# Attention in pairs of heads on the two row halves of the matmul array, with PSUM laid out anew

## The reference

```
z = RMSNorm(x) @ W_in                    # split into qA kA vA qB kB vB
A: 8 q heads, 2 kv heads, head dim 64, own 64-row chunk + 2 chunks before, learned sink per head
B: 8 heads, head dim 64, own chunk + 8 chunks before, learned bias by relative distance
s = q k^T / 8 (+ bias), masked;  m = max(s, sink);  p = exp(s - m) / (sum + exp(sink - m))
x = x + W_out @ concat(RMSNorm_a(p_A v_A), RMSNorm_b(p_B v_B))
x = x + MoE(RMSNorm(x))                  # top-1 of 4 groups, then top-2 of 8 gated experts, FF 256
```

## Time and profile before

| | us |
|---|---|
| three timed runs | 1059.56, 1064.88, 1090.57 (median 1064.88) |
| the profiled execution | 1060.6 |
| its span, first to last instruction | 1058.8 |
| PE, DVE, ACT busy in the span | 1010.7, 395.1, 299.8 |
| mean granted clock of PE | 0.99 |

### The profile page before, as it was taken

How to read it: one execution, slowest core, us unless ns; L and a number is a source line. 1 busy time by engine, 2 the same in 40 slices (tenths; PEclk the granted TensorE clock), 3 DMA queues, 4 the chain that set the end, 5 groups by cost and what they waited for, 6 DMA issues and landing times. The chain is left out here.

```text
span 1058.8 us, 16244 instructions
## 1 busy us (share of the span) xinstructions
PE 1010.7 (95%) x6187; PEld 521.7 (49%) x6187; DVE 395.1 (37%) x1155; ACT 299.8 (28%) x866; POOL 89.3 (8%) x72
## 2 busy tenths in 40 slices
PE   6999999999899999999999999998999999988995
PEld 3444555454485455465655556578544333333331
DVE  0343233342555546364555546358231111111110
ACT  1221222221435435353544535220111111111110
POOL 1000000000200000000000000000221221111111
PEclk9999999999999999999999999999999999999998
DMA  9510111100281101011010301076589999999972
GB/s 356 196 40 1 40 40 40 40 13 27 100 300 45 60 1 61 13 48 39 23 60 1 148 33 60 2 301 257 204 298 353 391 389 387 389 387 388 383 267 41
DMA packets 34439, 164.64 MB, mean 155 GB/s; under 512 B 7808, under 2 KB 9888, under 8 KB 20928
## 3 DMA queue, kind: packets, MB, share of 16 engines
q1 hardware_dynamic: 24192, 134.92, 32.1%
q0 software_dynamic: 6912, 17.32, 6.6%
q10 hardware_dynamic: 3264, 11.44, 2.8%
HBM read 147.10 MB, written 24.41 MB: 162 GB/s over the span
## 5 line engine op out<-in xcount | busy, mean ns | idle before, releaser
L1260 PE MATMUL ps<-arena 128*128 128x512 f32 (+1 forms) x640 | 252.2, 554 | 8.2 <-DMA arena<-in_w_in 8.2
L1260 PEld LDWEIGHTS ps<-arena 128*128 128x128 f32 x640 | 121.4, 191 | 133.9 <-issue 129.6
L1510 PE MATMUL ps<-arena 128*32 128x512 f32 x1536 | 171.9, 598 | 10.6 <-DMA arena<-in_wexp 9.2
L1342 PE MATMUL ps<-arena 64*128 64x256 f32 (+4 forms) x384 | 123.2, 421 | 0.0
L1423 PE MATMUL ps<-arena 128*128 128x512 f32 x256 | 120.6, 592 | 0.0
L942 DVE COPY arena<-ps 128x128 f32<-128x128 f32 (+2 forms) x144 | 53.7, 373 | 166.4 <-PE ps L1354 165.5
L784 ACT ACTIVATE arena<-arena 128x256 f32<-128x256 f32 (+6 forms) x144 | 84.0, 583 | 90.0 <-DVE arena L1027 89.7
L1510 PEld LDWEIGHTS ps<-arena 128*32 128x32 f32 x1536 | 49.9, 110 | 114.9 <-issue 113.0
L1342 PEld LDWEIGHTS ps<-arena 64*128 64x128 f32 x384 | 59.0, 185 | 74.4 <-DVE arena L1027 46.3
L1528 PE MATMUL ps<-arena 128*32 128x512 f32 x768 | 87.2, 592 | 0.7 <-ACT arena L841 0.7
L1023 DVE CUSTOM_DVE_ANT_0 arena<-ps,arena 128x256 f32<-128x256 f32 (+6 forms) x144 | 77.5, 538 | 2.6 <-PE ps L1342 1.9
(11 more groups left out here) (162 smaller groups left out, 870.0 us busy)
## 6 DMA issues: line engine op xcount, KB each, us to landing
arena<-in_wexp SPq DMA_DIRECT2D x96, 1024.0 KB, 24.6
arena<-in_x SPq DMA_DIRECT2D x18, 512.0 KB, 4.5
arena<-in_w_in ACTq DMA_DIRECT2D x3, 2048.0 KB, 23.0
arena<-in_xT SPq DMA_DIRECT2D x9, 512.0 KB, 3.6
arena<-in_w_out SPq DMA_DIRECT2D x1, 4096.0 KB, 13.9
out_y<-arena SPq DMA_DIRECT2D x8, 512.0 KB, 2.6
h_rows<-arena SPq DMA_DIRECT2D x8, 512.0 KB, 3.0
arena<-in_bias SPq DMA_DIRECT2D x1, 2560.0 KB, 9.1
```

What stands on the lines that cost most here:

```text
L1260: ins = mm(bank(Z_BANK[c], 0, CHUNK[c]), xt[:, j, k, :], w_in[:, a:a + CHUNK[c]], start=(k == 0), stop=(k == KD - 1))
L1342: ins = mm(ps[:, at:at + step], q, kt[:, col:col + step], start=True, stop=True)
L1510: ins = mm(bank(s % 2)[u:u + UNIT], xgt[:, s % 2, k, u:u + UNIT], ring[expert_of(s, q) % RING][:, k * 512:(k + 1) * 512], start=(k == 0), ...
```

## The change

Units run over t, then pairs of heads, then m, then the two heads of the pair: two units in a row are two heads of one mixer, and v counts the 72 pairs. The heads of A are paired over the two kv heads (h and h+4), with sinks, gains and w_out's rows reordered on the host. `scores(v)` makes both heads' scores, alternately from partitions 0 to 63 and 64 to 127, into different banks; A and B share banks 1 and 2, and where one of them is over 512 wide the scores wait for all earlier biasing. PSUM: banks 0 to 3 scores, 4 and 5 transposed probabilities (4 also the pair's output, transposed back), 7 the values' sum, 6 alone the stage behind, except in the last tiles. Each pair is divided at once; each head has its own exp of the sink.

```diff
+        o_ps = bank(4, 3 * P, 4 * P)
+        pv_ps = bank(7, 0, P)
+        def scores_at(m, r, width):
+            if m == 0:
+                return (640, 1024)[r]
+            return 0 if r == 0 else 2048 - max(width, 512)
...
-        units = [(t, m, h) for t in range(NT) for h in range(HEADS) for m in (0, 1)]
+        units = [(t, m, 2 * p + r) for t in range(NT) for p in range(4) for m in (0, 1) for r in range(2)]
...
-        BUSY = ({19: 22, 21: 3, 22: 2}, {7: 2, 9: 3, 19: 20, 21: 9, 22: 8})
+        BUSY = ({21: 20, 23: 3, 24: 2}, {9: 2, 12: 3, 21: 20, 23: 9, 24: 8})
...
 ACT
+            for v in range(NV + 3):
+                pair_out(v - 3)
+                copy_pt(2 * v - 2)
+                probs(2 * v + 2)
+                if v % 8 == 3 and v >= 8:
+                    squares_out(v // 8 - 1)
+                pieces(act_pieces, 2 * v)
+                copy_pt(2 * v - 1)
+                probs(2 * v + 3)
+                pieces(act_pieces, 2 * v + 1)
             squares_out(NT - 1)
...
 DVE
+            def divide(v):
+                dve.wait_ge(s_p, 2 * v + 2)
...
+                    link(nc.vector.reciprocal(r2, s2))
+                dve.wait_ge(s_ob, v + 1)
+                dve.wait_ge(s_pt, min(2 * v + 6, NU))
...
-                if g in (13, 17):
+                if g in (15, 18):
...
+            for v in range(NV + 3):
+                copy_pt(2 * v - 2)
+                biased(2 * v + 2)
+                pieces(dve_pieces, 2 * v)
+                divide(v - 3)
+                copy_pt(2 * v - 1)
+                biased(2 * v + 3)
+                if v % 8 == 3 and v >= 8:
+                    norm_out(v // 8 - 1)
+                pieces(dve_pieces, 2 * v + 1)
             norm_out(NT - 1)
...
 PE
+            def scores(v):
...
+                if v >= 1:
+                    wide = unit_info(2 * v - 1 if m == 0 else 2 * v)[5] > 512
+                    if wide or v >= 2:
+                        pe.wait_ge(s_sp, 2 * v if wide else 2 * v - 2)
...
+                for i in range(len(runs)):
+                    for r in range(2):
+                        a = r * HD
...
+                        ins = mm(ps[:, at:at + step], q, kt[:, col:col + step], start=True, stop=True)
+                        if i == len(runs) - 1:
+                            ins.then_inc(s_qk[r], 1)
...
+                pe.wait_ge(s_ott, v + 1)
+                pe.wait_ge(s_ptv, min(2 * v + 5, NU))
+                if v >= 1:
+                    pe.wait_ge(s_on, v)
+                nc.tensor.transpose(o_ps, outt[:, v % 2], ident).then_inc(s_ob, 1)
...
+                if t < NT - 1 and g in (12, 13, 14, 16, 17, 18):
+                    n = (g - 12) // 4
+                    at = g - 12 - 4 * n
...
+                    if g == 16:
+                        pe.wait_ge(s_x2, 2 * t + 1)
+                    for c in range(3 * at, min(3 * at + 3, KD)):
+                        ins = mm(bank(6), ot[:, c], w_out[:, c, 512 * n:512 * n + 512], start=(c == 0), stop=(c == KD - 1))
...
+                if g in (21, 22):
+                    half = g - 21
+                    if half == 0:
+                        pe.wait_ge(s_h2, t + 1)
+                    elif t < NT - 2:
+                        pe.wait_ge(s_h2a, t + 1)
...
+            for v in range(NV + 3):
...
+                transpose_probs(2 * v - 2)
+                scores(v + 1)
+                pieces(pe_pieces, 2 * v)
+                pair_back(v - 3)
+                transpose_probs(2 * v - 1)
+                pieces(pe_pieces, 2 * v + 1)
+                values(v - 2)
+                if 1 <= v < FIRST_OUT:
+                    keep_busy(5 - v // 4, 6)
```

More of the change, by code:

```diff
@@ L772, in act_pieces @@
                     rstd(rs2, ss2).then_inc(s_s2, 1)
-                if g == 20:
+                if g == 21:
                     act.wait_ge(s_t2, 2 * t + 1)
                     nc.scalar.activation(h2t[:, 0:4], bank(6).rearrange("p (g c) -> p g c", g=4), ACT.Copy).then_inc(s_h2a, 1)
[L777 to L794, removed]
-                copy_pt(u)
-            pair_out(NU - 1)
+            probs(0)
+            probs(1)
+            for v in range(NV + 3):
[8 more added lines that the diff above has]
+                pieces(act_pieces, 2 * v + 1)
             squares_out(NT - 1)
-            for u in range(NU, NU + 24):
+            for u in range(NU + 6, NU + 25):
                 pieces(act_pieces, u)
@@ L954, in divide @@
[L954 to L962 removed]
+                    dve.wait_ge(s_pv[u % 2], u // 2 - 1)
@@ new lines, in copy_pt @@
+                assert all(x[2] == P for x in tiles[:cut])
+                nc.vector.tensor_copy(pt_of(u)[:, 0:cut * P], bank(4, 0, cut * P)).then_inc(s_ptv, 1)
+            def divide(v):
+                if not 0 <= v < NV:
+                    return
+                t, m, h = units[2 * v]
+                c = stat_at(m, h)
+                dve.wait_ge(s_p, 2 * v + 2)
+                r2, s2 = rden[:, c:c + 2], psum_e[:, t % 2, c:c + 2]
+                if m == 0:
+                    dve.wait_ge(s_es, v + 2)
+                    link(nc.vector.tensor_tensor(r2, s2, esink[:, h:h + 2], ALU.add))
+                    link(nc.vector.reciprocal(r2, r2))
+                else:
+                    link(nc.vector.reciprocal(r2, s2))
+                dve.wait_ge(s_ob, v + 1)
+                dve.wait_ge(s_pt, min(2 * v + 6, NU))
+                a = 512 * m + h * HD
+                nc.vector.tensor_tensor(row[:, t, a:a + P].rearrange("p (h c) -> p h c", c=HD),
+                                        o_ps.rearrange("p (h c) -> p h c", c=HD),
+                                        r2.unsqueeze(2).broadcast_to([P, 2, HD]), ALU.mult).then_inc(s_on, 1)
@@ L1004, in dve_pieces, with biased @@
                     ins.then_inc(s_lt, 1)
-                if g == 23:
+                if g == 24:
                     dve.wait_ge(s_lg, t + 1)
-                    nc.vector.tensor_tensor(logits[:, t], bank(7, 0, NR), rbias, ALU.add).then_inc(s_rv, 1)
-            for u in range(NU):
+                    nc.vector.tensor_tensor(logits[:, t], bank(6, 256, 256 + NR), rbias, ALU.add).then_inc(s_rv, 1)
+            def biased(u):
+                if u >= NU:
+                    return
                 t, m, h, segs, tiles, width = unit_info(u)
-                k = u % 16
                 c = stat_at(m, h)
@@ L1028, in _ @@
                                         ALU.mult).then_inc(s_sp, 1)
[L1029 to L1048 removed]
+            biased(0)
+            biased(1)
+            for v in range(NV + 3):
[8 more added lines that the diff above has]
+                pieces(dve_pieces, 2 * v + 1)
             norm_out(NT - 1)
[L1050 to L1051 removed]
             dve.wait_ge(s_rload, 16 * 10)
@@ L1095, in choose_second @@
                 tt_(mb[:, t0:t1], eq_, wide(c_valid[:, t0:t1].unsqueeze(2), NE), ALU.mult).then_inc(s_mb, 1)
-            for u in range(NU + 10, NU + 24):
+            for u in range(NU + 6, NU + 25):
                 pieces(dve_pieces, u)
```

287 lines of the change are left out of this document (117 added, 170 removed).

## The result

The changed kernel takes 1050.6 us (median of four runs, 1049.8 to 1052.4) for 1064.5 before; the ratio is 0.989 (95% interval 0.986 to 0.992). It is a ratio of means, without one execution of before that ran in a slower state (1090.6 us). 1050 was predicted, and no difference beyond 2%. Its profiled execution took 1051.3 us, span 1049.5, mean granted clock 0.97.

The account below looks back on a forecast made before the run. It took attention to be bound by PE's own instruction stream. With serial waits counted, tiles 1 to 3 gave -4.6, -2.3, -2.8, four steady tiles -1.3 each, the drain +4.1: -10.8 us from 1060.6, so 1050, range 1016 to 1084.

Parts of the forecast that it names:

- Term 1: Score passes on PE: even and odd heads stream together on two row halves, 83 us becoming 42, 41 us less work.
- The fear for runs of 128 columns: Weight loads leave these runs no gain; each of 16 wide B pairs would lose 0.2 us, 3 us in all.
- Term 2: Switches to the half-array form on PE: 72 visits instead of 144, 0.26 us each, 19 us saved, bounds 14 and 26.
- PE's own work: PE's instruction stream in attention falls by 60 us of 392; a steady tile from 49.1 to about 41.
- Term 3: Attention turns: new serial waits on DVE and ACT give time back; steady tiles take 47.8 us, gaining 1.3, not 8.
- Term 4: Drain from tile 8 to its transposes: w_out, residual chain and fillers come later, 64.5 us for 60.4, 4.1 us lost.
- The third rival: PE's clock falls in the new waits: 28 us slower, 1078 us; chance 0.05.
- The first rival: DVE's and ACT's turns hide behind PE, so only PE's work counts: 1005 us, or 1028 with half the waits; chance 0.21.
- The second: Rival: row halves take turns on PE instead of overlapping while the waits stay: 1087 us; chance 0.12.

Follow-up runs that it names:

- the parted run: Changed kernel with a full-array filler product between all even-head and all odd-head score passes of each pair: 1107.4 us, ratio 1.042 to the kernel before.
- e9: e7 plus, in the turn behind the squares, DVE's h2 moved ahead of the even head's bias: 1038.4 us, ratio 0.975 to the kernel before.
- the two drain runs: Changed kernel with 4 fillers instead of 20 ahead of tile 7's h2 transposes: 1045.9 us; with DVE's norm of tile 8's mixer also moved later: 1043.5 us.
- e10: e9 plus 4 fillers instead of 20 ahead of tile 7's h2 transposes and DVE's late norm: 1033.0 us, ratio 0.971 to the kernel before.
- e4: Changed kernel with eight filler products before the pair-back where the residual's squares hold ACT, for projections of tiles 0 to 2: 1048.7 us, ratio 0.987.
- e7: Changed kernel with the residual's squares on ACT moved ahead of the odd head's exp: 1047.2 us, ratio 0.984 to the kernel before.
- the run with the heads in turn: Changed kernel with the two loops of `scores` swapped, all even-head passes issued before the odd head's: 1050.0 us, ratio 0.988 to the kernel before.
- the few-fillers run: Changed kernel with the fillers ahead of tile 7's h2 transposes cut from 20 products to 4: 1045.9 us, ratio 0.984 to the kernel before.

## Why the prediction was right, and where only its sum was

- **Term 1** (83 us of score streaming to 42) is right, and shown: two heads take 1.29 us where one takes 1.28. The fear for runs of 128 columns, taken from the Trainium skill, "TensorE: Matmul & The Clock Gate", LDWEIGHTS, did not come true here: with a run of 512 and one of 128 a pair still costs what one head does.
- **Term 2** is right in kind, and 0.26 us a visit was not too much. The 0.2 of 1.28 us for passes of 1.08 is in the changed kernel what it was before, but it leaves out the way in and out; the second visit of the parted run costs 0.29 to 0.38, where the bounds were 0.2 and 0.36. What the 72 visits less gave in the whole is not isolated.
- **PE's own work** in a steady tile was put at 41.6 us by the list of turns; it is 42.8. Over all of attention it was to fall by 60 us, and the page shows 36 us less busy time; but the clock kept back up to 16 us in tiles 1 to 3 and 8 (an estimate by the windows: 0.06x30.6 + 0.08x43.3 + 0.04x44.4 + 0.12x73.6).
- **Term 3** named the right places: the eight turns of tile 6 (from one start of scores to the next) are 8.25, 8.25, 4.9, 4.9 for w_out, 5.5 for the squares, 5.8 for the router and 4.35 and 4.6 around the mixer's transposes, where 8.2, 8.2, 4.9, 4.9, 5.8, 6.1, 4.7, 4.7 stood. The waits were oversized: 6.2 us a steady tile (47.8 - 41.6), measured 3.7. (The list with waits adds up to 47.5, not 47.4.) Steady tiles gained 2.7 to 3.1 each instead of 1.3, 11.2 us instead of 5.2. The new wait of scores for DVE's bias, the first thing that the term named, is 0.2 us a tile; ACT's queue and h2 on DVE are what PE waits for.
- **Term 4** named the right mechanism, the fillers ahead of the h2 transposes, the squares ahead of pair-out and the copy ahead of the mixer's squares, and undersized it: 18.0 us from w_out to tile 8's transposes for 15.7. Both missing amounts lie where the clock was low: the fillers took 6.26 us, not 4.5 (4.63 in e9, where they ran at full clock), and from the end of DVE's copy to those transposes it took 3.9, not 2.7.

```profile
670.00:680.00 10.00, 8.37 (x51) 5.93 (x50) 2.87 (x7) 2.09 (x6) 0.00 (x0) 0.86 0.36 122
680.00:691.20 11.20, 7.69 (x60) 7.15 (x59) 2.79 (x6) 2.32 (x7) 0.00 (x0) 0.82 1.01 411
```

  That DVE's copy stands behind the norm and the router waits for it was in the sum; the two drain runs show that 7 us of the drain, this wait among them, can be avoided. The larger miss lies ahead of the drain: from the start of tile 8 to w_out's end 55.6 us (617.6 to 673.2) for 48.8. e10, at full clock and with squares and h2 early, needs 51.1 there (608.2 to 659.35).
- **The third rival**, the clock, was partly true, and the forecast had nothing for it. Tile 2 gained 0 of 2.3 and tile 3 1.6 of 2.8; e4 takes 2.7 us off these two tiles and e7 4.0, clock and wait together; tile 3 at full clock with the waits unchanged (the run with the heads in turn) is 1.0 shorter. In tile 8 the windows of the changed kernel read

```profile
630.00:640.00 10.00, 8.27 (x56) 4.80 (x54) 5.53 (x20) 5.70 (x20) 0.00 (x0) 0.81 0.34 118
640.00:650.00 10.00, 9.64 (x74) 7.36 (x74) 6.98 (x27) 4.92 (x20) 0.00 (x0) 0.68 0.10 42
```

  by which (0.19 + 0.32) x 10, some 5 us of PE's work, were lost. That amount is worked out and no run isolates it; with squares and h2 early and the short drain tile 8 ran at 1.00.
- **The first rival** (waits hide) falls: a steady tile has 3.7 us of waits, and 3.4 still with both links of its longest chain moved. **The second** (no overlap) falls by the trace; parted heads, with the second visit, cost 48.7 us.

So the overlap, the serial turns and the drain were named rightly, but that 1050 came out is luck, as errors cancelled: steady tiles gave 6.0 us more than forecast and tile 1 gave 0.4 more; tiles 2 and 3 gave 3.5 less, and tile 8 with the drain 9.1 less (+13.2 for +4.1). Tile 0, counted at nothing, shows 4.7 us less (17.5 for 22.2). Together that is 9.3 us for 10.8. Two causes are likely for tile 0, neither tested: the windows are cut at each tile's first exp, and in the new order the exps of a pair run further ahead of PE's pieces, a shift that tile 8's window pays back; and the changed kernel runs fewer fillers there (55 passes for 78, with 32 for 16 in tile 1).

## What to carry to other kernels

When an engine's work is cut by pairing, list its turns and see which chain of the other engines ends each: here the longest wait, in one turn of eight, came of a chain through ACT and DVE. Moving one link only renamed the wait; moving both renamed it again and made it shorter. Look for the idle time of the waiting engines ahead of the late instruction and put the long independent operation there. Look at the granted clock beside the waits: most of what these two moves gained came off in tiles where it had fallen. Fillers that keep the clock up must stand where PE waits anyway and not outlast that wait, and not between a ready operand and its use.

## What was not expected of the hardware

- Passes on the two row halves overlapped in whichever order the program has them: with the even head's four passes ahead of the odd head's four, the eight took 1.36 us, as when alternated (1.35). An operation on the whole array between them parted them (2.97 us for the turn).
- The granted clock fell in tiles 1 to 3 of the changed kernel but not in tiles 4 to 7, which have the same waits, somewhat shorter. With the same instructions in tiles 1 to 7, the few-fillers run had 1.00 in tile 1 for 0.94 and 0.96 in tile 2 for 0.92: where it falls differs from one execution to the next, by about 0.7 us in tile 1.
- e4's tile 4 and e7's tile 5 fell to 0.96 and 0.93 and took 2.0 and 2.2 us longer, though PE's waits there had been filled or shifted, not added (some 0.4 us of e4's is the fillers outlasting the wait). What decides it is not settled.
